# Three attention stages of a fused two-block kernel, with the turns, value products and outputs one step further behind the scores

## The chip, the cores and the metric

The kernel runs on one core of a Trainium2 chip. The time is device microseconds (us) of one execution; for the kernel before it is 2418.43 us, the median of three runs (2418.36 to 2418.55). Nothing in it is split over cores, so one span is the whole time.

## The reference, cut to what matters

The program computes two transformer-like blocks one after the other for 256 tokens of width 1024 in float32: layers with several mixers, and at the end two large layers of experts. Three places in it are softmax attention over 256 keys, with 128 queries to a tile:

```python
# differential attention (8 heads, key width 32, value width 64)
p = softmax(where(kpos <= qpos, q @ k.T * scale, -inf))      # two maps per head
o = (p[:, :, 0] - lam * p[:, :, 1]) @ v
# attention over 256 memory tokens (4 heads, width 64)
o = softmax(q @ k.T * 64 ** -0.5) @ v
# selected and windowed attention (8 heads, width 64); at 256 tokens both are causal
o = gate1 * (softmax(s_selected) @ v_selected) + gate2 * (softmax(s_window) @ v_window)
# latent attention (16 heads, key width 96, value width 64), masked by positions
o = softmax(q @ k.T * 96 ** -0.5) @ v
```

## The kernel before, in words

Everything is float32. Activations stay on chip; weights are streamed from memory by SyncE. The stages follow each other, with a barrier between two of them (line 111). `attention(steps, ...)` at line 992 is one such stage and is called three times. In this text they are **stage A** (line 1948; differential attention, then memory attention), **stage B** (line 2501; memory attention, then selected and windowed attention) and **stage C** (line 3988; latent attention).

A stage is a list of steps, and each step has two score tiles of 128 queries. With 128 keys (`nk`, the first query tile of a causal head) a step is called **short** here, with 256 keys **long**.

- Stage A: 20 steps. Steps 0 to 15 are differential, short and long in turn (even ones short, odd ones long); their two maps are joined into one before the turn, so they have one row (`rows(w)` is 1). Steps 16 to 19 are memory steps: long, two rows.
- Stage B: 20 steps. Steps 0 to 3 are memory steps; steps 4 to 19 have two rows each and are short (even) and long (odd) in turn. Beside them runs a small compressed attention (`cmp_att_pe`, `cmp_att_act`, `cmp_att_dve`) in the iterations 0 to 6, and `gate_rows` puts two multiplications on VectorE in the iterations 15 and 16.
- Stage C: 16 long steps with two rows each, all alike.

Each engine has its own loop, written out in program order, and executes it in that order. In words, for a loop index s:

- TensorE (lines 1018 to 1055): **scores** of step s (line 1027; two products, into one of four score banks, three in stage B), then the **turn** of step s - TURN (line 1042; a 128 by 128 transpose per row and key tile), then the **value** product of step s - VALUE (line 1053). The scores wait until the bank's last user has been read (`maxed`). The turn waits for the exponentials of its step (`exped`) or, in a differential step, for its join (`joined`). The value product waits for `pt_ready`, the copy of its turned probabilities.
- ScalarE (lines 1060 to 1078): the two **exponentials** of step s (line 1069), and then the **copy** of the turned probabilities of step s - TURN out of the accumulator bank (line 1077).
- VectorE (lines 1114 to 1148): the first score tile of step s is scaled, masked and its maximum taken (line 1097); the reciprocal of the sums of step s - 1 (line 1125, waits for both its exponentials); the first **output** row of step s - OUT (line 1108 or 1110); in stage A the ratio (line 1131), in stage B the gate factor (line 1137); the second score tile of step s (line 1097); the join of step s - 1 (line 1144); the second output row.

TURN, VALUE and OUT are 2, 3 and 4 where a differential step is in the list (stage A), else 1, 2 and 3 (stages B and C). The exponentials of four steps fit in the ring `slot`, and the per-row maxima, sums, reciprocals and ratios of four steps in `st`, a ring of 8 columns. No line of this function starts a DMA or uses GpSimd.

The loop of ScalarE, which decides much of the order:

```python
if s < N:
    for x in range(2):
        act.wait_ge(maxed, 2 * s + x + 1)
        ...  # exponential x of step s
if s >= TURN:
    j = s - TURN
    act.wait_ge(turned, j + 1)
    ...  # copy of the turned probabilities of step j, then pt_ready
```

Of the kernel before, what the change touches and what calls it, by code (L numbers as in the profile page):

```python
# [12 lines left out]
ACT = mybir.ActivationFunctionType  # L13
# [3 lines left out]
P = 128  # L17
# [9 lines left out]
M_HEADS, HD = 4, 64  # L27
# [70 lines left out]
def build(nc, I, out, upto=99):  # L98
# [5 lines left out]
    def sem(name):  # L104

        of_stage.append(nc.alloc_semaphore(name))
        return of_stage[-1]
# [86 lines left out]
    zone = Zone()  # L194
    bank_pair = nc.alloc_psum_tensor("bank_pair", [P, 2, 512], F32)
    banks = [bank_pair[:, i, :] for i in range(2)] + [nc.alloc_psum_tensor(f"bank{i}", [P, 512], F32) for i in range(2, 8)]
# [137 lines left out]
    class Modulation:  # L334
# [4 lines left out]
        total = 2 * EARLY_TILES  # L339
# [652 lines left out]
    def attention(steps, score_banks=(0, 1, 6, 7), beside=None):  # L992
# [3 lines left out]
        if not stage():  # L996
# [4 lines left out]
        SB = len(s_bank)  # L1001
        also = beside or {}
        pt_sb = [zone("probs_t", [P, 4, P]) for _ in range(2)]
        st = zone("softmax_stats", [P, 4, 8])
        neg_max, total, inv, ratio = (st[:, x, :] for x in range(4))
        scored, maxed, exped, joined, turned, pt_ready, pv_done, out_done = (
            sem(f"att{n}_{x}") for x in ("scored", "maxed", "exped", "joined", "turned", "pt_ready", "pv_done", "out_done"))
        N = len(steps)
        any_joined = any(w["lam"] is not None for w in steps)
        TURN, VALUE = (2, 3) if any_joined else (1, 2)  # L1010
        OUT = VALUE + 1
        rows = lambda w: 1 if w["lam"] is not None else 2
        outs_by = [sum(rows(w) for w in steps[:s + 1]) for s in range(N)]
# [2 lines left out]
        with StageBlock() as block:  # L1016
# [40 lines left out]
            @block.scalar  # L1057
            def _(act):
                f = act_f.on(act)
                for s in range(N + TURN):  # L1060
                    if "act" in also:
                        also["act"](f, act, s)
                    if s < N:
                        w = steps[s]
                        for x in range(2):
                            u = 2 * s + x
                            act.wait_ge(maxed, u + 1)
                            e = slot(s, x)[:, 0:w["nk"]]
                            f(nc.scalar.activation(e, e, ACT.Exp, bias=neg_max[:, u % 8:u % 8 + 1], scale=-1.0,
                                                   accum_out=total[:, u % 8:u % 8 + 1]), exped, wait=False)  # L1070
                    if s >= TURN:
                        j, w = s - TURN, steps[s - TURN]
                        act.wait_ge(turned, j + 1)
                        if j >= 2:
                            act.wait_ge(pv_done, j - 1)
                        c = rows(w) * w["nk"]
                        f(nc.scalar.activation(pt_sb[j % 2][:, :, :].rearrange("p a b -> p (a b)")[:, 0:c],
                                               banks[2 + j % 2][:, 0:c], ACT.Copy), pt_ready, wait=False)

            @block.vector  # L1080
            def _(dve):
                f = dve_f.on(dve)
                inverted = {}
                outs = [0]

                def score(s, x):
                    w, u = steps[s], 2 * s + x
                    if x == 0:
                        dve.wait_ge(scored, s + 1)
                        if s >= 4:  # L1090
                            dve.wait_ge(turned, s - 3)
                    got, out = s_bank[s % SB][:, x * S:x * S + w["nk"]], slot(s, x)[:, 0:w["nk"]]
                    mask = w["mask"][x] if type(w["mask"]) is list else w["mask"]
                    if mask is None:
                        got, out = (a.rearrange("p (a b) -> p a b", b=P) for a in (got, out))
                        mask = causal[:, 0:P].unsqueeze(1).broadcast_to([P, w["nk"] // P, P])
                    f(nc.vector.tensor_tensor_reduce(out, got, mask, scale=-w["scale"], scalar=3.0e38, op0=ALU.add, op1=ALU.min,
                                                     accum_out=neg_max[:, u % 8:u % 8 + 1]), maxed, wait=False)

                def out(j, x):  # L1100
                    w, u = steps[j], 2 * j + x
                    if x == 0:
                        dve.wait_ge(dve_order, inverted[j])
                        dve.wait_ge(pv_done, j + 1)
                    got, by = banks[4 + j % 2][:, x * HD:(x + 1) * HD], inv[:, u % 8:u % 8 + 1]
                    if w["add"][x]:
                        dve.wait_ge(out_done, outs[0])
                        ins = nc.vector.scalar_tensor_tensor(w["out"][x], got, by, w["out"][x], ALU.mult, ALU.add)
                    else:
                        ins = nc.vector.tensor_scalar(w["out"][x], got, by, None, ALU.mult)  # L1110
                    f(ins, out_done, wait=False)
                    outs[0] += 1

                for s in range(N + OUT):
                    if "dve" in also:
                        also["dve"](f, dve, s)
                    if s < N:
                        score(s, 0)
                    r = s - 1
                    now = steps[r] if 0 <= r < N else None  # L1120
                    j = s - OUT
                    pair = slice(2 * r % 8, 2 * r % 8 + 2)
                    if now is not None:
                        dve.wait_ge(exped, 2 * r + 2)
                        inverted[r] = f(nc.vector.reciprocal(inv[:, pair], total[:, pair]), wait=False)
                    if j >= 0:
                        out(j, 0)
                    if now is not None and now["lam"] is not None:
                        a = 2 * r % 8
                        dve.wait_ge(dve_order, inverted[r])  # L1130
                        ready = f(nc.vector.scalar_tensor_tensor(ratio[:, a:a + 1], total[:, a:a + 1], now["lam"], inv[:, a + 1:a + 2],
                                                                 ALU.mult, ALU.mult), wait=False)
                    if now is not None and now["coef"] is not None:
                        o, coef = now["coef"]
                        part = slice(2 * r % 8 + o, 2 * r % 8 + 2)
                        dve.wait_ge(dve_order, inverted[r])
                        inverted[r] = f(nc.vector.tensor_tensor(inv[:, part], inv[:, part], coef, ALU.mult), wait=False)
                    if s < N:
                        score(s, 1)
                    if now is not None and now["lam"] is not None:  # L1140
                        a = 2 * r % 8
                        e0, e1 = (slot(r, x)[:, 0:now["nk"]] for x in range(2))
                        dve.wait_ge(dve_order, ready)
                        f(nc.vector.scalar_tensor_tensor(e0, e1, ratio[:, a:a + 1], e0, ALU.mult, ALU.add), joined, wait=False)
                    if j >= 0 and rows(steps[j]) == 2:
                        out(j, 1)
                    if "gate" in also:
                        also["gate"](f, dve, s, out_done)
# [790 lines left out]
    for h in range(B_HEADS):  # L1939
        for t in range(NT):  # L1940
# [4 lines left out]
                              scale=B_DK ** -0.5, mask=causal[:, S - nk:S], lam=lam[:, 2:3], coef=None,  # L1945
                              add=(False, False),
                              out=[mix[:, t, 512 + h * B_DV:512 + (h + 1) * B_DV]] * 2))
    attention(steps + memory_steps(0, MQT, mix[:, :, 1024:1280]))
    def even_output():

# [461 lines left out]
    for h in range(D_HEADS):  # L2412
        g = h // (D_HEADS // D_GROUPS)
        for t in range(NT):
# [3 lines left out]
                              scale=HD ** -0.5, mask=causal[:, S - nk:S], lam=None,  # L2418
# [74 lines left out]
    def gate_rows(f, dve, i, out_done):  # L2493
# [3 lines left out]
        if i == 16:  # L2497
            dve.wait_ge(out_done, 24)
            f(nc.vector.tensor_tensor(mix[:, :, 512:768], mix[:, :, 512:768], P1[:, :, 2840:3096], ALU.mult), wait=False)

    attention(steps, score_banks=(0, 1, 6), beside=dict(pe=cmp_att_pe, act=cmp_att_act, dve=cmp_att_dve, gate=gate_rows))

    def mods(base):
# [1229 lines left out]
    def latent_input():  # L3733
# [22 lines left out]
        with StageBlock() as block:  # L3756
# [153 lines left out]
            def _(dve):  # L3910
# [68 lines left out]
                for h0, h1 in ROPE_HEADS:  # L3979
# [6 lines left out]
    latent_input()  # L3986
    AO = QN[:, :, :, :].rearrange("p t h d -> p (t h d)")[:, 0:NT * D].rearrange("p (t n) -> p t n", t=NT)
    attention([dict(qT=[QTM[:, h, t * P:(t + 1) * P] for t in range(NT)], kT=[KTM[:, h, :]] * 2, nk=S,
                    v=[[VN[:, k, h * V_HEAD:(h + 1) * V_HEAD] for k in range(NT)]] * 2, scale=QK ** -0.5,
                    mask=[pmask[:, t, :] for t in range(NT)], coef=None, lam=None,  # L3990
# [111 lines left out]
```

## Time and profile before

| | us |
|---|---|
| median of three runs | 2418.43 |
| the profiled execution | 2416.78 |
| its span (first to last instruction) | 2415.5 |
| stage A, 145.5 to 186.0 | 40.5 |
| stage B, 344.5 to 393.3 | 48.8 |
| stage C, 1466.5 to 1505.0 | 38.5 |

Over the span TensorE's matmuls are busy for 2334.5 us (97%), its weight loads for 1908.5 us (79%), VectorE for 1863.8 us (77%), ScalarE for 1154.1 us (48%), GpSimd for 177.8 us (7%). The DMA engines moved 429.26 MB. The stage borders are read from the first scores product and the last output row. How to read it: the three stages are about 5% of the time, so a share of the whole span tells little of them, and each is to be read from a window of its own. A matmul's duration includes its pipeline, so durations of neighbouring matmuls overlap; the distance from one group's start to the next group's start is the real rate.

### The profile page before, as it was taken

To read this page: it belongs to the slowest core of one execution; us is meant where nothing else is said; L and a number is where in the kernel's file an instruction comes from. 1 tells how busy PE (TensorE), PEld (TensorE's weight loads), DVE (VectorE), ACT (ScalarE), POOL (GpSimd) and SP (SyncE) were. 2 spreads that over 40 slices of the span, in tenths; PEclk is the share of its full clock that TensorE was granted. 3 is DMA by queue.
4 is the path that set the end of the run, shared out by engine and by line. 5 is a ranking of instruction groups with operands and counts; after the bars stand their busy time and mean duration, and the time that the engine had idled before them with its cause. 6 is when DMAs were issued, how large, how long until landed. Compare 5 with 4: busy or idle time off the path is not lost. (4 is left out here: it accounts for less than half of the span.)

```text
span 2415.5 us, 37030 instructions
## 1 busy us (share of the span) xinstructions
PE 2334.5 (97%) x11673; PEld 1908.5 (79%) x11673; DVE 1863.8 (77%) x4229; ACT 1154.1 (48%) x1992; POOL 177.8 (7%) x204
## 2 busy tenths in 40 slices
PE   7989999999999999999999999999999999999997
PEld 5766467868787888888888867787788888888886
DVE  6677776778997788888888855699877777777776
ACT  5674247332485544444444436317744444444443
POOL 1000000001470000000000000026400000000000
PEclk9999999999999999999999999999999999999999
DMA  6524641572215677776677741411255555555553
GB/s 257 194 104 149 240 161 36 195 268 78 79 36 173 235 260 250 253 257 251 252 260 252 252 171 70 148 53 45 88 198 189 189 191 188 191 188 192 188 190 137
DMA packets 144609, 429.26 MB, mean 178 GB/s; under 512 B 15230, under 2 KB 21374, under 8 KB 144510
## 3 DMA queue, kind: packets, MB, share of 16 engines
q1 hardware_dynamic: 144510, 428.08, 50.5%
q8 instruction: 45, 0.74, 0.1%
q14 instruction: 54, 0.44, 0.0%
HBM read 426.99 MB, written 1.05 MB: 177 GB/s over the span
## 5 line engine op out<-in xcount | busy, mean ns | idle before, releaser
L3484 PE MATMUL bank<-v_parts,weighted_high 128*128 128x512 f32 x1952 | 528.4, 392 | 0.5 <-DVE weighted_low L3627 0.5
L3470 PE MATMUL bank<-h_t_parts,u_t_high 128*128 128x512 f32 x1824 | 450.5, 389 | 0.0
L3484 PEld LDWEIGHTS bank<-v_parts,weighted_high 128*128 128x128 f32 x1952 | 351.1, 189 | 65.3 <-issue 2.6
L3470 PEld LDWEIGHTS bank<-h_t_parts,u_t_high 128*128 128x128 f32 x1824 | 342.4, 188 | 71.0
L3548 ACT ACTIVATE u_t_high<-u_ring 128x1024 fp32r<-128x1024 f32 x228 | 242.0, 1061 | 181.3 <-DMA u_ring<-in_peer_u 179.1
L3567 ACT ACTIVATE activated<-activated 128x256 f32<-128x256 f32 x228 | 95.4, 418 | 475.9 <-DVE activated L3615 475.9
L3602 DVE TENSOR_TENSOR u_t_low<-u_ring,u_t_high 128x1024 fp32r<-128x1024 f32 x228 | 278.6, 1222 | 31.8 <-ACT u_t_high L3548 23.8
L3484 PE MATMUL bank<-v_parts,weighted_low 128*128 128x512 f32 x976 | 301.5, 390 | 0.0
L3609 DVE TENSOR_TENSOR v_parts<-v_ring,v_parts 128x1024 fp32r<-128x1024 f32 x242 | 294.0, 1215 | 3.3 <-ACT v_parts L3555 3.3
L3555 ACT ACTIVATE v_parts<-v_ring 128x1024 fp32r<-128x1024 f32 x242 | 255.1, 1054 | 48.2 <-PE bank L3484 46.8
L3473 PEld LDWEIGHTS bank<-h_t_parts,u_t_low 128*128 128x128 f32 x1824 | 248.8, 190 | 17.8
L3473 PE MATMUL bank<-h_t_parts,u_t_low 128*128 128x256 f32 x1824 | 254.4, 282 | 0.0
L3615 DVE TENSOR_REDUCE activated<-bank 128x256 f32<-128x512 f32 x228 | 156.9, 688 | 87.8 <-PE bank L3473 86.6
L3484 PEld LDWEIGHTS bank<-v_parts,weighted_low 128*128 128x128 f32 x976 | 183.3, 188 | 39.9
L3625 DVE CAST weighted_high<-activated 128x256 fp32r<-128x256 f32 x244 | 71.9, 295 | 134.8 <-PE bank L3484 133.4
L3621 DVE TENSOR_TENSOR activated<-activated,gates 128x256 f32<-128x256 f32 x256 | 106.9, 418 | 10.1 <-ACT activated L3560 9.3
L3627 DVE TENSOR_TENSOR weighted_low<-activated,weighted_high 128x256 fp32r<-128x256 f32 x244 | 103.8, 425 | 8.3
L3293 POOL TENSOR_SCALAR onehot_pool<-iota_row,slot_e,slot_gate 128x128 f32<-128x128 f32 x128 | 101.1, 791 | 52.9 <-PE bank_pair L3309 28.9
L3590 POOL TENSOR_TENSOR x_res<-x_res,gated_sum 128x512 f32<-128x512 f32 x2 | 3.3, 1640 | 1353.9 <-DVE gated_sum L3666 1353.9
L3336 ACT ACTIVATE onehot<-onehot,slot_gate 128x128 f32<-128x128 f32 x256 | 87.4, 392 | 0.1
L3269 DVE TENSOR_TENSOR onehot<-bank,slot_e 128x512 f32<-128x512 f32 x128 | 86.9, 679 | 0.0
L3637 DVE SCALAR_TENSOR_TENSOR late_tiles<-late_tiles,bank_pair 128x1024 f32<-128x1024 f32 x70 | 84.9, 1213 | 0.0
(601 smaller groups left out, 3460.3 us busy)
## 6 DMA issues: line engine op xcount, KB each, us to landing
v_ring<-in_peer_v SPq DMA_DIRECT2D x244, 512.0 KB, 3.4
u_ring<-in_peer_u SPq DMA_DIRECT2D x228, 512.0 KB, 4.6
panel<-in_l_w_in SPq DMA_DIRECT2D x15, 2048.0 KB, 8.4
late_tiles<-in_ada_w SPq DMA_DIRECT2D x54, 512.0 KB, 4.4
mod_ring<-in_ada_w SPq DMA_DIRECT2D x42, 512.0 KB, 4.5
panel<-in_peer_w_q SPq DMA_DIRECT2D x8, 2048.0 KB, 7.7
panel<-in_l_w_out SPq DMA_DIRECT2D x4, 2560.0 KB, 9.0
early_u<-in_peer_u SPq DMA_DIRECT2D x20, 512.0 KB, 3.4
```

What stands on the lines that cost most here:

```text
L3293: nc.gpsimd.tensor_scalar(O1P[:, n % R4, :], iota[:, :], slot_e1[:, tok], slot_g[:, tok], ALU.is_equal, ALU.mult).then_inc(pool_hot, 1)
L3470: nc.tensor.matmul(banks[2 + k][:, :], UTH[:, k, j, :], H2[:, j, :, :].rearrange("p a s -> p (a s)"), start=(j == 0), stop=False, skip_gro ...
L3473: last = nc.tensor.matmul(banks[2 + k][:, 0:S], UTL[:, k, j, :], H2[:, j, 0, :], start=False, stop=(j == KD - 1), skip_group_check=True)
L3484: last = nc.tensor.matmul(banks[4 + 2 * t + half][:, :], w[:, t * P:(t + 1) * P], v[k][:, half * 512:(half + 1) * 512], start=opens and n ...
L3548: nc.scalar.activation(UTH[:, s, :, :].rearrange("p a b -> p (a b)"), UR[:, s, :], ACT.Copy)\
L3555: nc.scalar.activation(VH[s], slot, ACT.Copy).then_inc(v_high, 1)
L3567: nc.scalar.activation(AA[:, s, :], AA[:, s, :], ACT.Gelu).then_inc(gelued, 1)
L3602: nc.vector.tensor_tensor(UTL[:, s, :, :].rearrange("p a b -> p (a b)"), UR[:, s, :], UTH[:, s, :, :].rearrange("p a b -> p (a b)").bitcas ...
L3609: nc.vector.tensor_tensor(VL[s], v_slot(b, s)[0], VH[s].bitcast(F32), ALU.subtract)\
L3615: nc.vector.tensor_reduce(AA[:, s, :], banks[2 + s][:, :].rearrange("p (a s) -> p s a", a=2), AX.X, ALU.add).then_inc(summed, 1)
L3621: nc.vector.tensor_tensor(AA[:, s, :], AA[:, s, :], g, ALU.mult).then_inc(w_full, 1)
L3627: nc.vector.tensor_tensor(low[:, :], AA[:, s, :], high[:, :].bitcast(F32), ALU.subtract)\
```

## The change

TURN and VALUE become 3 and 4 in stage A and 2 and 3 in the stages B and C; OUT stays VALUE + 1 and so rises by one as well. The ring of small statistics has 16 columns in place of 8. On TensorE the turn and the value product of a step are issued one iteration later, on ScalarE the copy, on VectorE the outputs; the loops of the engines run one iteration more at the end. The ring of exponentials (four steps), the turned probabilities (two steps) and the banks stay as they are.

```diff
-        st = zone("softmax_stats", [P, 4, 8])
+        st = zone("softmax_stats", [P, 4, 16])
...
-        TURN, VALUE = (2, 3) if any_joined else (1, 2)
+        TURN, VALUE = (3, 4) if any_joined else (2, 3)
...
-                            f(nc.scalar.activation(e, e, ACT.Exp, bias=neg_max[:, u % 8:u % 8 + 1], scale=-1.0,
-                                                   accum_out=total[:, u % 8:u % 8 + 1]), exped, wait=False)
+                            f(nc.scalar.activation(e, e, ACT.Exp, bias=neg_max[:, u % 16:u % 16 + 1], scale=-1.0,
+                                                   accum_out=total[:, u % 16:u % 16 + 1]), exped, wait=False)
...
-                                                     accum_out=neg_max[:, u % 8:u % 8 + 1]), maxed, wait=False)
+                                                     accum_out=neg_max[:, u % 16:u % 16 + 1]), maxed, wait=False)
...
-                    got, by = banks[4 + j % 2][:, x * HD:(x + 1) * HD], inv[:, u % 8:u % 8 + 1]
+                    got, by = banks[4 + j % 2][:, x * HD:(x + 1) * HD], inv[:, u % 16:u % 16 + 1]
...
-                    pair = slice(2 * r % 8, 2 * r % 8 + 2)
+                    pair = slice(2 * r % 16, 2 * r % 16 + 2)
...
-                        a = 2 * r % 8
+                        a = 2 * r % 16
...
-                        part = slice(2 * r % 8 + o, 2 * r % 8 + 2)
+                        part = slice(2 * r % 16 + o, 2 * r % 16 + 2)
...
-                        a = 2 * r % 8
+                        a = 2 * r % 16
```

## Rows read from the trace of the kernel before

**Rows 1.** Stages A, B, C: length; PE, PEld, DVE, ACT, POOL busy us; clock; DMA share, GB/s

```profile
145.50:186.00 40.50, 31.88 (x200) 26.17 (x200) 27.45 (x156) 27.90 (x101) 0.00 (x0) 1.00 0.16 53
344.50:393.30 48.80, 43.89 (x310) 38.19 (x310) 29.38 (x172) 31.54 (x104) 0.00 (x0) 1.00 0.10 39
1466.50:1505.00 38.50, 35.85 (x257) 32.88 (x258) 20.18 (x113) 28.01 (x82) 0.00 (x0) 1.00 0.16 56
```

**Rows 2.** TensorE's waits, stages A, A, B, C: us in total, times, longest

```profile
PE bank L1042 <- DVE h_t L1144: 4.9, 8, 1.3
PE bank L1053 <- ACT probs_t L1077: 3.0, 9, 0.5
...
PE bank L1042 <- ACT h_t L1069: 3.4, 7, 0.8
...
PE bank L1042 <- ACT h_t L1069: 1.3, 2, 0.8
```

**Rows 3.** Timeline of stage A: start, us, engine, line, tiles [idle before]

```profile
150.76 0.43 PE L1053 MATMUL bank<-even_in,probs_t 128*128 128x64 f32 x2
151.03 0.66 PE L1027 MATMUL bank_pair<-even_in,b_q_t 128*128 128x128 f32 x4
...
164.09 1.08 PE L1027 MATMUL bank<-even_in,b_q_t 128*128 128x256 f32 x4
...
166.69 0.33 PE L1042 MATMUL bank<-ident,h_t 128*128 128x128 f32 x1 [0.63 <-DVE h_t L1144]
166.91 0.36 ACT L1077 ACTIVATE probs_t<-bank 128x256 f32<-128x256 f32 x1
...
167.32 0.66 PE L1053 MATMUL bank<-even_in,probs_t 128*128 128x64 f32 x4 [0.31 <-ACT probs_t L1077]
...
167.82 1.08 PE L1027 MATMUL bank_pair<-even_in,b_q_t 128*128 128x256 f32 x4
...
168.17 0.26 ACT L1077 ACTIVATE probs_t<-bank 128x128 f32<-128x128 f32 x1
```

**Rows 4.** Timeline of stage A: scores of its last step, and its last output rows

```profile
178.89 1.08 PE L1027 MATMUL bank<-mem_k_t,even_in 128*128 128x256 f32 x4
...
185.66 0.48 DVE L1110 TENSOR_SCALAR mix<-bank,softmax_stats 128x64 f32<-128x64 f32 x2 [0.48 <-PE bank L1053]
```

**Rows 5.** Timeline of stage B: one pair of steps from scores to scores

```profile
375.63 1.08 PE L1027 MATMUL bank_pair<-d_k_t,d_q_t 128*128 128x256 f32 x4
...
376.75 0.42 DVE L1097 CUSTOM_DVE_ANT_0 h_t<-bank_pair,causal_mask 128x256 f32<-128x256 f32 x1 [1.16 <-PE bank_pair L1027]
...
377.89 0.51 ACT L1069 ACTIVATE h_t<-h_t,softmax_stats 128x256 f32<-128x256 f32 x1
...
378.55 0.66 PE L1042 MATMUL bank<-ident,h_t 128*128 128x128 f32 x4 [0.27 <-ACT h_t L1069]
...
379.44 1.08 PE L1027 MATMUL bank_pair<-d_k_t,d_q_t 128*128 128x256 f32 x4
```

**Rows 6.** Timeline of stage B: a copy 512 wide, its value product, the next scores

```profile
365.14 0.57 ACT L1077 ACTIVATE probs_t<-bank 128x512 f32<-128x512 f32 x1
...
365.77 1.10 PE L1053 MATMUL bank<-odd_in,probs_t 128*128 128x64 f32 x8
...
366.71 0.66 PE L1027 MATMUL bank<-d_k_t,d_q_t 128*128 128x128 f32 x4
```

**Rows 7.** Timeline of stage B: last scores, last turn, last output rows

```profile
387.04 1.08 PE L1027 MATMUL bank_pair<-d_k_t,d_q_t 128*128 128x256 f32 x4
...
389.95 0.66 PE L1042 MATMUL bank<-ident,h_t 128*128 128x128 f32 x4 [0.77 <-ACT h_t L1069]
...
392.49 0.60 DVE L1108 SCALAR_TENSOR_TENSOR mix<-bank,softmax_stats,mix 128x64 f32<-128x64 f32 x2 [0.80 <-PE bank L1053]
```

**Rows 8.** Timeline of stage C: scores of two neighbouring steps

```profile
1476.77 1.08 PE L1027 MATMUL bank_pair<-k_heads_t,q_heads_t 96*128 96x256 f32 x4
...
1478.96 1.08 PE L1027 MATMUL bank<-k_heads_t,q_heads_t 96*128 96x256 f32 x4
```

## The prediction

> **What bounds the kernel now.** I read the busy times of the three attention stages in windows of their own first, since together they are 127.8 us of a span of 2415.5 and the page's averages tell nothing of them. A is 40.5 us with matmuls busy for 31.9, B 48.8 with 43.9, C 38.5 with 35.9; the granted clock is 1.00 in all three, and GpSimd is idle [rows 1]. So TensorE is nearest to its limit in C and has most idle time in A. Next, TensorE's own waits by stage: ahead of turns (L1042) it waits 4.9 us for joins in A, 3.4 us for exponentials in B and 1.3 us in C; ahead of value products (L1053) it waits 3.0 us for the copies in A [rows 2]. Then the timelines, to see which of these waits closes a loop, because only that one sets the pace.
>
> The steady pattern repeats every two steps in A and B (a short and a long one). In A, from the scores of a long step to those of the next long one, it takes 167.82 - 164.09 = 3.73 us. TensorE stands 0.63 us ahead of a turn at 166.69, and then again 0.31 us ahead of the value product at 167.32, which waits for the copy of 166.91. The copy stands on ScalarE behind both exponentials of the long step [rows 3]. The loop is: scores, 2.82 us to the start of the copy (first tile, second tile, its exponential), 0.41 for the copy, 0.50 for the value product of four products, and the next long scores. 2.82 + 0.41 + 0.50 = 3.73. The turn's wait is inside the time in which TensorE would wait for the copy anyway.
>
> In B a pair takes 379.44 - 375.63 = 3.81 us and the loop is another one: scores at 375.63, second exponential at 377.89, its end releases the turn of the same step at 378.55, and turn and a value product of four take 0.89 to the next long scores: 2.26 + 0.51 + 0.15 + 0.89 = 3.81 [rows 5]. The copy there is 256 wide and ready in time. In C TensorE's instructions follow each other without a gap, 1478.96 - 1476.77 = 2.19 us for a step [rows 8].
>
> **The change, part by part.** The ring of 16 columns renames addresses; the same instructions have the same sizes: 0 us. No DMA, nothing of SyncE or GpSimd is in this function, so no queue of theirs is passed. One more iteration of each loop adds no instruction; what it costs is in the ends below. The turn waits for data one step older, so the waits of L1042 go. But the value product of iteration s has always needed the copy that ScalarE issues in iteration s - 1, behind the exponentials of step s - 1: with VALUE = TURN + 1 that is the same distance after the change. **The copy loop keeps its length in steps, and only the sizes in it change.** In A and B steps alternate, so moving copy and value by one step swaps a short step for a long one, and the reverse.
>
> *Stage A.* Behind the long exponentials now stands the copy of a short step (0.26 in place of 0.36, so 0.31 with the hand-over in place of 0.41) and its value product of two products: 151.03 - 150.76 = 0.27 in place of 0.50 [rows 3]. The loop becomes 2.82 + 0.31 + 0.27 = 3.40, 0.33 less. The other half (the long copy behind short exponentials: the short step's last exponential ends at 168.17, 4.08 after the scores of 164.09, plus 0.41) lets the value product start 4.49 after the long scores; the scores of the next long step at 3.40, with 0.92 of their own and 0.11 for a single transpose, end at 4.43. (0.92 is the step of 2.19 in C less its value of eight, 0.94 less 0.10 for the restart after a wait, and less its turn of four transposes, 0.44: the 0.89 of [rows 5] less 0.45 for the value of four behind it.) It just fits, so it adds nothing. Six such pairs: -1.9 us by step 15. In the memory steps one more pair gives 0.3, and a four-product value moves behind the last scores: these come 2.7 earlier than at 178.89 [rows 4]. Then a turn of four (0.44) and a value of eight (0.84) more than before stand between them and the last outputs (185.66): A = -1.4 us. Bounds: 0, if the neighbouring chains on VectorE hold the 3.73, and -2.7, if the ends give nothing back. I take -1.4, from the rows' own terms.
>
> *Stage B.* Here the swap goes the wrong way. Behind the long exponentials now stands a copy of a long step, 512 wide, and a value of eight products: from the copy's start to the product 365.77 - 365.14 = 0.63, from there to the next scores 366.71 - 365.77 = 0.94 [rows 6]. The copy starts 2.26 + 0.51 = 2.77 after the scores [rows 5]. 2.77 + 0.63 + 0.94 = 4.34 us for a pair against 3.81, so +0.53, though the turn's wait is gone; TensorE's own work in a pair is 3.81 less the wait of 0.27 and the start-up behind it, about 3.4, so it idles for 0.9 ahead of that one product. VectorE and ScalarE are not later than before: the second exponential needs only its scores. Steps 0 to 6 are ordered by the compressed attention, whose work waits for VectorE; I count gain and loss there as equal, except that a memory step's value of eight now stands ahead of the scores of step 7 where four stood: +0.3. From step 7 to step 19 there are six pairs: +3.2. The end: before, from the last scores to the last outputs 392.49 - 387.04 = 5.45. After: 3.40 to the value of step 17, 0.94 to the last turn, and from a last turn to the last outputs 392.49 - 389.95 = 2.54 [rows 7]: 6.88, +1.4. B = +4.9 us. The operations are all in the trace; the wait of an eight-product value behind a long copy in steady state is not. Below, a pair stays at 3.81 (another chain overlaps it): B = +1.7. Above, each pair pays a further 0.1 for hand-over: +5.5. I take +4.9, since each of its terms has a row.
>
> *Stage C.* All steps are equal, so nothing is swapped. The loop needs at most 2.77 + 0.63 + 0.84 = 4.24 in two steps, TensorE's work is 4.38: it stays the bound, 2.19 a step. At the start a third pair of scores fills the first turn's wait (0.8 of the 1.3 in rows 2), but the first value product now waits for a copy behind the exponentials of step 2, and takes that back. At the end the value of step 13 waits 0.7 for the copy behind the last exponentials, where before the last turn waited 0.5. C = +0.3; between -1.3 (all waits of rows 2 go) and +1.4 (an end as in B).
>
> What follows a stage starts when it ends, and TensorE waits for no large transfer there, so I carry the sums through whole. **Sum: -1.4 + 4.9 + 0.3 = +3.8 us.** The profiled execution took 2416.78 us (span 2415.5 and 1.3 around it), 1.65 below the median of the runs; against the median of 2418.43 the sum gives 2422.2 us.
>
> **The rivals.** *(1) The gaps go.* The waits of L1042 are TensorE's largest repeated gaps; if each shortens the stage by itself, the change gives 4.9 + 3.4 + 1.3 = 9.6 us [rows 2]: 2408.8 us. For it: VectorE and ScalarE are under 75% busy in every stage [rows 1]. Against it: the 0.31 us at 167.32 that follows the turn's wait, in A itself [rows 3], says what is late next, and the same order of ScalarE holds in B. The Trainium skill, "Perfetto Trace Analysis", section Optimization Strategy, says to find the gaps on the engine in question, see which semaphore ends them, and make that dependency start sooner; by that alone this rival would be the forecast. Chance 0.06.
>
> *(2) Nothing moves.* The pairs of B stay at 3.81 or less because the copy is hidden after all, A gains its 1.4 and the ends take it back: 2418.4 us, some 1 us to either side. For it: only five per cent of the time is touched. Against it: the order copy after exponentials is written in the code. Chance 0.15.
>
> *(3) Slower beyond the bound.* B loses as forecast and A has no gain, because the long copy behind the short exponentials has only 0.06 us of slack (4.43 against 4.49 above): if VectorE's first tile of the long step is later by more than that, the value product of the long step decides there and each pair of A stays at 3.73 or grows. Then 4.9 + 0.3 and up to 1 us of A's longer end: +5.2 to +6.2, 2424.1 us. It decides from the point where that product starts over 0.3 later than 4.49 after its scores. Chance 0.17.
>
> *(4)* My case, 0.62: 2420 to 2424, likeliest 2422.2.
>
> **How the numbers follow.** 0.2%, about what a measurement of this kernel can tell from no change, is 4.8 us: 2413.6 to 2423.3. Faster by more: rival 1 and hardly anything else, with little of its chance below the bound short of its full sum: 0.05. Slower by more: rival 3 (0.15 of its 0.17) and the upper end of my case (0.05): 0.20. Within: 0.75. The range for 8 in 10 takes my case with its bounds, the upper half of rival 2 and most of rival 3: 2418.6 to 2424.2.
>
> **What the changed profile would show.** In A a pair at 3.40, no wait ahead of turns, a value product of two products released by a 128 wide copy. In B a pair at 4.34 with TensorE idle 0.8 to 0.9 ahead of a value of eight products, released by the copy of 512, and no wait ahead of turns but at the ends. In C steps at 2.19. Stage lengths 39.1, 53.7 and 38.8. The forecast is wrong if B's pair is at 3.4 to 3.8 (then the copy is not in its loop), if A stays at 3.73, or if the time between the stages changes by over 1 us.

## The result, and the profile after

The changed kernel takes 2422.64 us (median of 17 runs, 2419.62 to 2425.77) against 2418.20 us for the kernel before in the same comparison (17 runs, 2415.66 to 2421.70). The medians differ by 4.4 us, and the ratio is 1.0019 (0.19% slower), 95% interval 1.0012 to 1.0026, or 2.9 to 6.3 us. The median is within 0.5 us of the forecast of 2422.2 us, and the sign is the one that was forecast. The ratio is just within the 0.2% that I had called "same"; the upper end of its interval lies beyond.

The profiled execution took 2419.62 us, span 2418.4 (2416.78 and 2415.5 before). From here on a stage's length runs from its first scores (in B from the scores of the compressed attention that precede them) to the start of its last output rows. This is a narrower measure than the windows of rows 1.

| us | stage A | stage B | stage C | pair in A | pair in B | step in C |
|---|---|---|---|---|---|---|
| before | 39.87 | 47.70 | 37.19 | 3.73 | 3.80 | 2.19 |
| changed | 38.56 | 52.34 | 37.45 | 3.40 | 4.34 | 2.20 |
| forecast of the difference | -1.4 | +4.9 | +0.3 | -0.33 | +0.53 | 0 |
| measured difference | -1.3 | +4.6 | +0.3 | -0.33 | +0.54 | 0 |

The three stages add 3.6 us, the span 2.9 us. The 0.7 us between them is in a stretch that the change does not touch (last section).

The three stages of the changed kernel in windows (length, then busy us of TensorE's matmuls and weight loads, VectorE, ScalarE and GpSimd, granted clock, DMA); they answer to [rows 1]:

```profile
145.50:184.70 39.20, 31.46 (x200) 25.67 (x200) 27.55 (x156) 28.15 (x101) 0.00 (x0) 1.00 0.16 55
343.40:396.60 53.20, 43.53 (x310) 38.25 (x310) 30.11 (x172) 30.68 (x104) 0.00 (x0) 1.00 0.09 34
1469.10:1507.90 38.80, 36.02 (x257) 32.90 (x258) 20.29 (x113) 27.84 (x82) 0.00 (x0) 1.00 0.16 55
```

The instruction counts and nearly the busy times are those of before; B is 4.4 us longer with the same work in it. So the time is waiting. TensorE's waits in the stages A, B and C of the changed kernel (us in total, times, longest), which answer to [rows 2]:

```profile
PE bank L1053 <- ACT probs_t L1077: 5.9, 10, 1.4
PE bank L1042 <- DVE h_t L1144: 1.1, 2, 0.7
...
PE bank L1053 <- ACT probs_t L1077: 6.3, 9, 1.3
PE bank L2439 <- DVE cmp_probs L2487: 2.4, 1, 2.4
...
PE bank L1053 <- ACT probs_t L1077: 1.4, 2, 0.8
```

The change did what it says: waits ahead of turns (L1042) fell from 4.9 to 1.1 us in A, and from 3.4 and 1.3 us to nothing in B and C. In their place stand waits ahead of value products (L1053) for the copy of the turned probabilities: from 3.0 to 5.9 us in A, from 0.3 to 6.3 in B, from none to 1.4 in C. The row of these waits in B of the kernel before:

```profile
PE bank L1053 <- ACT probs_t L1077: 0.3, 1, 0.3
```

The timeline of one pair in A of the changed kernel, long scores to long scores (start us, duration, engine, line, tiles, idle time before); it answers to [rows 3]:

```profile
162.75 1.08 PE L1027 MATMUL bank<-even_in,b_q_t 128*128 128x256 f32 x4
...
165.88 0.43 PE L1053 MATMUL bank<-even_in,probs_t 128*128 128x64 f32 x2 [0.65 <-ACT probs_t L1077]
...
166.15 1.08 PE L1027 MATMUL bank_pair<-even_in,b_q_t 128*128 128x256 f32 x4
...
166.84 0.36 ACT L1077 ACTIVATE probs_t<-bank 128x256 f32<-128x256 f32 x1
...
167.25 0.52 PEld L1053 LDWEIGHTS bank<-even_in,probs_t 128*128 128x128 f32 x4 [0.26 <-ACT probs_t L1077]
167.25 0.66 PE L1053 MATMUL bank<-even_in,probs_t 128*128 128x64 f32 x4
```

166.15 - 162.75 = 3.40 us, with a value product of two as its last piece, 0.27 ahead of the scores. The value of four at 167.25 starts 4.50 us after the scores of 162.75, as forecast (4.49). Its weight load waits for the copy of 166.84, so this product too comes a little later than TensorE could take it: by some 0.07 us, with the forecast's 0.92 for the scores and 0.11 for the transpose (166.15 + 1.03 = 167.18).

The same in B of the changed kernel; it answers to [rows 5, 6]:

```profile
375.95 1.08 PE L1027 MATMUL bank_pair<-d_k_t,d_q_t 128*128 128x256 f32 x4
376.87 0.60 PE L1042 MATMUL bank<-ident,h_t 128*128 128x128 f32 x4
...
377.31 0.56 PE L1053 MATMUL bank<-odd_in,probs_t 128*128 128x64 f32 x4
...
377.70 0.66 PE L1027 MATMUL bank<-d_k_t,d_q_t 128*128 128x128 f32 x4
...
378.20 0.38 PE L1042 MATMUL bank<-ident,h_t 128*128 128x128 f32 x2
378.21 0.51 ACT L1069 ACTIVATE h_t<-h_t,softmax_stats 128x256 f32<-128x256 f32 x1
...
378.72 0.58 ACT L1077 ACTIVATE probs_t<-bank 128x512 f32<-128x512 f32 x1
...
379.34 1.10 PE L1053 MATMUL bank<-odd_in,probs_t 128*128 128x64 f32 x8 [0.76 <-ACT probs_t L1077]
...
380.29 1.08 PE L1027 MATMUL bank_pair<-d_k_t,d_q_t 128*128 128x256 f32 x4
```

TensorE has issued everything that it is allowed to by 378.20 and then stands 0.76 us until the copy, which ScalarE could start only at 378.72 behind the long step's second exponential. The turned tile that is copied had been ready since the turn of 376.87, and the copy starts as the exponential ends (378.21 + 0.51 = 378.72), so it waits for no free buffer either. Eight products follow, and only then may the next scores start: 4.34 us.

### The profile page after: what moved, and what is told of

Its sections match the earlier page's. It is cut to its first block and busy times, and to the rows that moved or that the text cites. A ratio compares the mean times of both kernels' runs of the same rounds, so it can differ in the third digit from the quotient of the medians.

```text
span 2418.4 us, 37030 instructions
## 1 busy us (share of the span) xinstructions
PE 2328.7 (96%) x11673; PEld 1905.7 (79%) x11673; DVE 1865.0 (77%) x4229; ACT 1149.9 (48%) x1992; POOL 177.9 (7%) x204
```

## The experiments

The theory is that of the prediction: a value product needs the copy that ScalarE issued one iteration earlier behind both exponentials, and the change only swaps which sizes meet in that loop. The rival is that distance itself is the cost (or the ring is), whatever the sizes and wherever the copy stands. Three questions help to tell them apart: whether the stages act each by itself, whether the swap of sizes or the distance is the cause, and whether the copy's place on ScalarE closes the loop. Each stage's length is read from one profile per kernel. The times have the median of the kernel before beside them, from the same comparison; those with a moved copy are medians of 5 or 11 runs, and the other five are of one run each, so that there only the profile is used. The edits shown are against the changed kernel, with its ring of 16 columns, but for the doubled copies in the kernel before. All stage results stand together here.

| kernel | stage A | stage B | stage C | pair in A | pair in B | time (before) |
|---|---|---|---|---|---|---|
| ring of 16 alone | 39.87 | 47.70 | 37.19 | 3.73 | 3.80 | 2417.26 (2418.12) |
| change in A alone | 39.25 | 47.69 | 37.19 | 3.40 | 3.80 | 2417.79 (2418.87) |
| B one step further still | 39.49 | 49.70 | 37.46 | 3.40 | 3.67 | 2421.56 (2418.87) |
| changed, copies of B twice | 38.56 | 57.2 | 37.45 | 3.40 | 4.82 | 2427.38 (2418.12) |
| before, copies of B twice | 39.88 | 50.8 | 37.19 | 3.73 | 4.03 | 2419.38 (2418.12) |
| changed, copy first | 32.96 | 45.88 | 35.55 | 2.84 | 3.48 | 2409.95 (2418.87) |
| before, copy first | 34.78 | 49.53 | 40.10 | 3.17 | 4.00 | 2416.98 (2418.87) |
| changed, copy between | 34.53 | 48.8 | 36.18 | 2.84 | 3.67 | 2410.16 (2418.12) |

### The ring alone

```diff
-        TURN, VALUE = (3, 4) if any_joined else (2, 3)
+        TURN, VALUE = (2, 3) if any_joined else (1, 2)
```

> The kernel before with the ring of 16 columns alone, lags of before. Theory: only addresses change; A 39.9, B 47.7, C 37.2 us as before, to 0.1. Rival (the wider ring moves tiles of later allocation or conflicts in another way): a stage differs by over 0.3 us with the granted clock unchanged.

All three stages are as before to 0.01 us. The ring costs nothing in them, and the rest is the lags.

### The change in stage A alone

```diff
-        TURN, VALUE = (3, 4) if any_joined else (2, 3)
+        TURN, VALUE = (3, 4) if any_joined else (1, 2)
```

> Lags of the change in stage A alone, those of before in B and C. Theory (the copy of a turned tile stands behind two exponentials, and the change only swaps short and long in that loop): the stages do not touch each other, so A is 38.6 us from first scores to last outputs as in the changed kernel (39.9 before), B 47.7 and C 37.2 as before. Rival (a change of clock or of a transfer between the stages makes part of the difference): B or C differ from before by over 0.3 us although their code is that of before.

B and C are those of before to 0.01 us, so the stages do not touch each other. A's steady pair is 3.40, but A is 39.25, where 38.6 was expected: one pair at its start took 4.10. In that profile the granted clock is 0.75 from 150 to 155 us and 0.91 from 155 to 160, where it is 1.00 in the profile of the changed kernel with the same code. The window rows of this run:

```profile
145.00:150.00 5.00, 3.63 (x21) 2.92 (x21) 2.98 (x18) 4.09 (x13) 0.00 (x0) 1.00 0.87 298
150.00:155.00 5.00, 3.42 (x14) 2.76 (x15) 3.49 (x21) 3.21 (x14) 0.00 (x0) 0.75 0.33 125
155.00:160.00 5.00, 4.44 (x27) 3.66 (x27) 4.21 (x27) 3.95 (x17) 0.00 (x0) 0.91 0.02 3
```

So the gain in A is 1.3 us where the clock stays up, and 0.6 where it falls, and the pairs are the safer reading.

### Stage B one step further still

```diff
-        TURN, VALUE = (3, 4) if any_joined else (2, 3)
+        TURN, VALUE = (3, 4) if any_joined else (3, 4) if SB == 3 else (2, 3)
```

(`SB` is the number of score banks, 3 in stage B alone.)

> Stage B alone one step further still: turn 3 and value 4 steps behind the scores; A and C as in the change. Theory: the long exponentials have the copy of a short step behind them again (256 wide) and its value product of four, so the loop is 2.77 + 0.41 + 0.50 = 3.68 us for a pair, shorter than the 4.34 of the change and than the 3.81 of before; the first outputs come a step later, so B is about 48 us against 52.3. Rival (each step of distance costs in B, whatever its size): the pair stays at 4.34 or grows, and B is 53 us or more.

The pair is 3.67 against an expected 3.68, and faster than both 4.34 and the 3.80 of before. More distance from the same kind of edit undid the loss: what costs in the steady pairs is the swap of short and long, not the distance. Its timeline:

```profile
375.60 1.08 PE L1027 MATMUL bank_pair<-d_k_t,d_q_t 128*128 128x256 f32 x4
...
377.85 0.51 ACT L1069 ACTIVATE h_t<-h_t,softmax_stats 128x256 f32<-128x256 f32 x1
...
378.36 0.36 ACT L1077 ACTIVATE probs_t<-bank 128x256 f32<-128x256 f32 x1
...
378.77 0.66 PE L1053 MATMUL bank<-odd_in,probs_t 128*128 128x64 f32 x4
379.27 1.08 PE L1027 MATMUL bank_pair<-d_k_t,d_q_t 128*128 128x256 f32 x4
```

Behind the long exponential now stands a copy of 256, behind it a value of four. The length of B was a miss: 49.70 where I had expected about 48. The gain of a pair is there, but the first steps, which are interleaved with the compressed attention, took longer than in the changed kernel (5.90 and 4.78 us between the long scores where it has 5.31 and 4.56), and the granted clock was 0.87 from 350 to 355 us and 0.79 from 355 to 360. The share of each is open. A of this run (39.49) also has a slow pair at its start (4.35), with a clock of 0.73 from 150 to 155.

### Each copy of stage B twice

```diff
+        spare, spare_done = (zone("spare", [P, 512]), sem(f"att{n}_spare")) if SB == 3 else (None, None)
...
+                        if SB == 3:
+                            if j:
+                                act.wait_ge(spare_done, j)
+                            nc.scalar.activation(spare[:, 0:c], banks[2 + j % 2][:, 0:c], ACT.Copy).then_inc(spare_done, 1)
                         f(nc.scalar.activation(pt_sb[j % 2][:, :, :].rearrange("p a b -> p (a b)")[:, 0:c],
                                                banks[2 + j % 2][:, 0:c], ACT.Copy), pt_ready, wait=False)
```

In the changed kernel:

> The changed kernel with each copy of stage B done twice: once more into a spare tile, ahead of the real copy. Theory (in B the long copy is in the loop that sets the pace): the pair grows by the whole of one 512 wide copy, 0.5 to 0.6 us, from 4.34 to 4.85 to 4.95, and the short copy's second run (0.36) costs nothing; A and C as in the change. Rival (the loop is elsewhere, TensorE's wait ahead of the eight products only shows it): the pair grows by less than 0.2 or by both copies, 0.9.

In the kernel before:

> The same second copy in stage B of the kernel before. Theory: its loop of 3.81 us runs through the last exponential and the turn; the loop through the short copy is 2.77 + 0.41 + 0.50 = 3.68 and becomes 4.04 with 0.36 more, so the pair grows by only 0.2 to 0.3 (to 4.0 to 4.1), less than the short copy's own time and far less than the long one's. Rival (the copies are in the loop of before as in the changed kernel's): 4.2 or more.

In the changed kernel a pair grows by 0.48 (4.34 to 4.82). In its timeline the two copies start 0.48 apart:

```profile
376.34 0.58 ACT L1081 ACTIVATE spare<-bank 128x512 f32<-128x512 f32 x1
376.82 0.59 ACT L1082 ACTIVATE probs_t<-bank 128x512 f32<-128x512 f32 x1
```

So the pair grows by the distance of exactly one long copy; the second short copy (0.27 from 378.06 to 378.33 in the same pair) costs nothing. The expected band of 4.85 to 4.95 was a little high, because I took a copy's duration and not its distance to the next. In the changed kernel the long copy is in the loop, and the short one is not.

In the kernel before a pair grows by 0.23 (3.80 to 4.03), within the expected 4.0 to 4.1, but not for the expected reason. The expectation added the short copy's duration (3.68 + 0.36 = 4.04). The two short copies start only 0.27 apart (384.41 and 384.68), which by the same sum gives 3.95, and the value of four behind them shows no wait. TensorE waits 0.46 us ahead of the value of eight, for the doubled long copy (here L1028 are the scores, L1054 the value products, L1081 the spare copy and L1082 the real one):

```profile
380.32 0.66 PE L1028 MATMUL bank<-d_k_t,d_q_t 128*128 128x128 f32 x4
...
382.29 0.58 ACT L1081 ACTIVATE spare<-bank 128x512 f32<-128x512 f32 x1
...
382.77 0.58 ACT L1082 ACTIVATE probs_t<-bank 128x512 f32<-128x512 f32 x1
...
383.41 1.10 PE L1054 MATMUL bank<-odd_in,probs_t 128*128 128x64 f32 x8 [0.46 <-ACT probs_t L1082]
...
384.35 0.66 PE L1028 MATMUL bank_pair<-d_k_t,d_q_t 128*128 128x128 f32 x4
```

From short scores to short scores that is 1.97 + 0.48 + 0.64 + 0.94 = 4.03 us, the whole pair. With one copy the same path is 0.48 shorter, some 3.6, under the 3.80 of the loop through the turn. So the run shows that neither copy sets the pace in B of the kernel before, and that the number came out right by luck: the loop that closed at 4.03 is one that was not in the expectation.

### The copy ahead of the exponentials

In each iteration of ScalarE's loop the copy of step s - TURN is issued before the exponentials of step s:

```diff
                 for s in range(N + TURN):
...
+                    if s >= TURN:
+                        j, w = s - TURN, steps[s - TURN]
+                        act.wait_ge(turned, j + 1)
...
                     if s < N:
                         w = steps[s]
                         for x in range(2):
...
-                    if s >= TURN:
-                        j, w = s - TURN, steps[s - TURN]
-                        act.wait_ge(turned, j + 1)
...
```

With the lags of the change:

> The changed kernel with ScalarE's copy ahead of the two exponentials of its iteration, not behind them, in all three stages. Theory: the value product then needs a copy that is issued one iteration of exponentials earlier, the loop through the copy is gone, and what is late next decides: in B TensorE's own work, 3.4 us for a pair (4.34 with the change); in A VectorE's chain of both tiles, reciprocal and join, 2.9 to 3.1 us (3.40); C stays at 2.19 a step and loses its wait at either end, 1 us. Sum against the changed kernel: B -6 to -7, A -2 to -3, C -1, so about 2412.5 us, 0.2 to 0.3% below the kernel before. Rival (the exponentials get late behind the copy, since it waits for a turn behind the scores): B's pair stays over 4 us and the time is within 1 us of the changed kernel.

With the lags of before (the ring stays at 16 columns):

> The kernel before in its lags (2, 3 in A; 1, 2 in B and C), with the copy ahead of the exponentials; the ring stays at 16. Theory: B's loop before ran through the last exponential and the turn, not through the copy, so B's pair stays at 3.81 us and B at 47 to 48 us; in A the loop through the copy was the longest one, the next is the one through the join at about 3.3 us, so A falls from 39.9 to 37 to 38; C about the same. Sum about -2.5 us against before. Rival (the copy loop decides in B too in the kernel before): B's pair falls well below 3.81, by 0.3 or more.

With the lags of the change it takes 2409.95 us (five runs, 2408.09 to 2410.88), ratio 0.9965 to the kernel before, interval 0.9951 to 0.9978: faster than both kernels, by 8.9 us and by some 12.7. B's pair is 3.48 against 3.4 expected, A's 2.84 against 2.9 to 3.1; the expected 2412.5 was 2.5 too high, mostly since A fell by 5.6 us and not by 2 to 3 (its memory steps and its ends gained too), and C by 1.9 and not by 1. In its profile the three stages are together 10.4 us shorter than before, but the span only 6.8: the stretches from B to C and behind C, which no edit touches, are 1.7 and 1.8 us longer. Such stretches vary from profile to profile (the one behind C is 911.3 us before and 913.0 with the ring alone). TensorE's waits in B of this kernel:

```profile
PE bank L2439 <- DVE cmp_probs L2487: 2.4, 1, 2.4
PE bank L2433 <- PEq L118: 1.2, 1, 1.2
PE bank L600 <- PEq L118: 1.0, 1, 1.0
PE bank L1053 <- DVE mix L1108: 0.4, 1, 0.4
```

The 6.3 us for the copies are gone, and matmuls are busy for 42.84 of 46.5 us:

```profile
338.00:384.50 46.50, 42.84 (x310) 38.22 (x310) 30.21 (x172) 30.33 (x104) 0.00 (x0) 1.00 0.10 39
```

With the lags of before the same edit gives 2416.98 us (eleven runs, 2416.00 to 2422.44), ratio 0.9999 (0.9990 to 1.0008): nothing that can be told from no change. A gains 5.1 us, where 2 to 3 were expected (pair 3.17, expected 3.3), but B's pair goes from 3.80 to 4.00, where I had expected no change, and a step in C from 2.19 to 2.32, so that C loses 2.9 us. That is a miss, and its row shows why. The timeline of a pair in B (L1069 is the copy here and L1077 the exponential):

```profile
372.73 0.44 PE L1042 MATMUL bank<-ident,h_t 128*128 128x128 f32 x2
...
373.20 0.38 ACT L1069 ACTIVATE probs_t<-bank 128x256 f32<-128x256 f32 x1 [0.53 <-PE bank L1042]
...
373.48 0.50 ACT L1077 ACTIVATE h_t<-h_t,softmax_stats 128x256 f32<-128x256 f32 x1
...
373.97 0.49 ACT L1077 ACTIVATE h_t<-h_t,softmax_stats 128x256 f32<-128x256 f32 x1
```

With a lag of one step the turn itself waits for the last exponential of the step before, so the copy waits for the turn (0.53 us), and the new exponentials stand behind it. With a lag of two the turn is early and the copy ready when it is reached. Over the whole kernel the lag alone gives +4.4 us, the order alone about nothing, and both together -8.9. The stages differ in this. In A each half gains by itself (-1.3 and -5.1 us, both -6.9). In B and C each half loses by itself (+4.6 and +1.8, +0.3 and +2.9), and only both together gain (-1.8 and -1.6).

### The copy between the two exponentials

> The changed kernel with the copy between the two exponentials. Theory: the loop through the copy is back but shorter by one exponential and the second tile: in B 1.12 to the first tile, 0.47 to its exponential, 0.51 for it, then 0.63 and 0.94: 3.67 us for a pair, against 3.48 with the copy first; in A 2.7, which is under the VectorE chain's 2.85, so A as with the copy first; C at 2.19 a step. About 2411 us, 1 to 1.5 above the copy first. Rival (the copy ahead of the second exponential delays the first less, which counts more): B's pair at 3.4 and the time below the copy first.

The edit puts the same block behind the exponential of x = 0. B's pair is 3.67 as expected, A's 2.84. The time is 2410.16 us (five runs, 2408.49 to 2412.83; ratio 0.9965, 0.9951 to 0.9978), which cannot be told from the copy first, though I had expected 1 to 1.5 us more. In the profiles its stages are 5 us longer together, but a part of that may be the granted clock (0.95 in A and 0.97 in B, where the copy first has 1.00 in both), and its span is only 2.9 us longer (2411.6 and 2408.7); the five runs do not bear it out. Which of the two is better is open; the loop length of 3.67 is settled.

## Why the prediction was right

*What closes the loop.* The step that carried the forecast was that the value product of an iteration needs the copy issued one iteration earlier behind both exponentials, before and after the change, so that only the sizes in that loop change. For B of the changed kernel the timeline shows it, the doubled copy shows it by price (the pair grows by the 0.48 us that the copy was doubled by), and the copy moved ahead by removal (4.34 to 3.48). For A the timelines show it, and the moved copy: 3.73 to 3.17 with the lags of before, 3.40 to 2.84 with those of the change. That the loop of B in the kernel before is the one through the turn rests on its timeline; the doubled copy there only shows that neither copy sets that pace.

*Stage A.* Pair 3.40 as forecast. The length fell by 1.3, forecast 1.4: the last scores come 2.6 us earlier (forecast 2.7), and the end gives back 1.3. The 0.06 us in the other half, on which rival 3 rested, was called slack, but 4.49 against 4.43 is a wait: TensorE is ready before the copy is. It came as forecast (the value of four starts at 4.50), and the pair stays at the 3.40 that the other half gives.

*Stage B.* Pair 4.34 as forecast, from rows 5 and 6. The length was forecast 0.3 too high. Up to the scores of step 7 the stage is 0.1 us longer, where I had put +0.3 for the memory step's value of eight; from there to the last scores 3.2 as forecast; behind them 1.38, forecast 1.43.

*Stage C.* Steps at 2.20, and +0.26 for the stage against +0.3; its two new waits (1.4 us) replace the two old ones (1.3 us).

*The rivals.* Rival 1 (the gaps go, 2408.8 us) is refuted for this change: the gaps of L1042 fell from 9.6 to 1.1 us and the time rose. The Trainium skill's rule in "Perfetto Trace Analysis", section Optimization Strategy, to find the gaps and what ends them and make that dependency start sooner, led to the largest gap in the profile. In A that gap did not close the loop; in B it did, but the edit that removed it lengthened another loop. Read again on the changed kernel, where the gap waits for the copy, the same rule leads to the copy ahead of the exponentials, which with the change is 8.9 us faster than the kernel before. In this case the rule held where the gap was the last one in its loop and the edit made no other loop longer. Rival 2 (nothing moves) and rival 3 (A gains nothing) are refuted by the pairs.

*Against the median.* The mechanism was right stage by stage, but the nearness of the total (2422.2 and 2422.64) is in part luck. The stages add 3.6 us and were forecast at 3.8; the profiles differ by 2.9 and the medians by 4.4, and the interval of the ratio (2.9 to 6.3 us) can't tell these apart. The profiled execution of the changed kernel is the fastest of its 17 runs, with the highest mean clock (0.997).

## What to carry to other kernels

When engines run hand-ordered loops, follow one loop of waits all the way round and write its length in iterations: issuing a consumer later gives the loop no more time where its producer is issued later too. Where steps alternate in size, such a shift swaps which sizes meet in the loop, and may lose in one stage more than it gains in another (here +4.6 and -1.3 us). Before adding distance, look at what the hand-over instruction stands behind on its own engine: here moving one copy ahead of two exponentials made a loss of 4 us into a gain of 9.

## What was not expected of the hardware

**The granted clock falls in short stretches, not all of them in each profile.** After stage B the profile of the kernel before has a clock of 0.66 for 10 us, the profile of the changed kernel 1.00 in the same code. First the kernel before, then the changed one:

```profile
393.00:403.00 10.00, 9.26 (x25) 5.14 (x26) 5.88 (x15) 8.92 (x20) 0.00 (x0) 0.66 0.00 1
```

```profile
396.30:406.30 10.00, 7.16 (x29) 4.38 (x30) 5.88 (x15) 9.13 (x22) 0.00 (x0) 1.00 0.00 1
```

The two levels of the clock are 1.2 and 2.4 GHz, so 0.66 is a mean of both over these 10 us. Ahead of it TensorE did less in the changed kernel, which waits more in stage B. These are the last 10 us up to the first product behind stage B, before and changed:

```profile
383.40:393.40 10.00, 7.66 (x56) 6.76 (x56) 6.11 (x33) 5.71 (x20) 0.00 (x0) 0.99 0.01 2
```

```profile
386.70:396.70 10.00, 6.67 (x51) 5.80 (x51) 5.22 (x29) 4.80 (x18) 0.00 (x0) 1.00 0.01 2
```

Over the last 30 us its matmuls were busy for 26.8 us before and for 23.6 in the changed kernel. Of the ten profiles of this case the changed kernel's is the only one in which the clock does not fall in the 10 us behind stage B; the others have 0.66 to 0.83 there. Yet the changed kernel with the copies of B twice was less busy still ahead of it (20.4 of 30 us) and fell to 0.83. So what makes the clock fall is open. The price is read from the first product behind stage B to the first split product of the next stage: 393.42 to 401.51 is 8.09 us with the low clock, 396.70 to 404.10 is 7.40 with the full one. These 0.69 us are the difference between the stages' sum (+3.6) and the span (+2.9).

Over the 17 runs of the changed kernel the time goes roughly with the mean clock: the three runs at 0.997 took 2419.6 to 2419.9 us, the three at 0.993 took 2424.5 to 2425.8, and those between spread from 2420.0 to 2424.7 (the one at 0.992 took 2423.3). An effect of 1 us in a stage can therefore be read from the periods of a profile, but not from a few runs.
